# Gated delta rule: inverse of I + A with 16x16 diagonal blocks made on POOL for three steps in four

## What is computed

```python
# q, k, v [N,H,T,64], g (log-decay), beta [N,H,T]; chunks of c tokens
g = cumsum(g within the chunk)
decay = exp(where(i >= j, g_i - g_j, -inf))
a_low = where(i > j, (k*beta) @ k.T * decay, 0)
tmat = inverse(eye + a_low)                # unit lower triangular
u = tmat @ (v * beta);  w = tmat @ (k * beta * exp(g))
for each chunk:                            # the scan
    v_new = u - w @ state
    o = (q * exp(g)) @ state + (q @ k.T * decay) @ v_new
    state = state * exp(g_last) + k_dec.T @ v_new
```

## Time and profile before

| | |
|---|---|
| runs | 3808.23 us median of 3 (3802.79 to 3814.48) |
| profiled execution | 3801.48 us |
| its span | 3799.7 us |
| mean granted TensorE clock | 0.984 |
| PE busy | 3641.7 us (96%) |
| DVE, ACT, POOL busy | 1549.1, 1070.8, 1297.7 us (41%, 28%, 34%) |
| DMA | 173.19 MB, mean 46 GB/s |

### The profile page before, as it was taken

The page is one execution under the profiler, slowest core; times in us unless marked ns, Lnnn a source line. Parts: engine busy times, 40 slices in busy tenths (PEclk is TensorE's granted clock), DMA queues, the critical chain, the costliest instruction groups (busy, mean ns, idle before and its releaser), DMA issues. The chain is left out here.

```text
span 3799.7 us, 47903 instructions
## 1 busy us (share of the span) xinstructions
PE 3641.7 (96%) x19176; PEld 3016.4 (79%) x19176; DVE 1549.1 (41%) x2391; ACT 1070.8 (28%) x1817; POOL 1297.7 (34%) x876
## 2 busy tenths in 40 slices
PE   6999999999999999999999999999979999999998
PEld 5777878776898989888877787887867887777877
DVE  4332333343354535444574333333337224444433
ACT  3343333331333333333013111111121114443221
POOL 4221212124221221222345343433342435554543
PEclk9999999999999999999999999999989999999999
DMA  2000000002000000001131111111132111111122
GB/s 98 23 29 27 28 23 33 24 28 76 29 12 12 1 23 1 23 1 60 67 127 59 50 44 50 44 50 44 50 116 70 48 43 49 48 47 46 61 83 72
DMA packets 52699, 173.19 MB, mean 46 GB/s; under 512 B 6569, under 2 KB 13353, under 8 KB 49841
## 3 DMA queue, kind: packets, MB, share of 16 engines
q1 hardware_dynamic: 52528, 170.80, 13.1%
HBM read 151.25 MB, written 19.52 MB: 45 GB/s over the span
## 5 line engine op out<-in xcount | busy, mean ns | idle before, releaser
L303 PE MATMUL DP<-XH,WH 128*128 128x512 f32 x2608 | 896.4, 425 | 21.7 <-POOL WL L251 20.5
L249 POOL CAST WH<-WRAW 128x1024 fp32r<-128x1024 f32 (+2 forms) x257 | 263.8, 1026 | 1638.3 <-issue 1041.5
L303 PE MATMUL DP<-XL,WH 128*128 128x512 f32 x2608 | 812.3, 393 | 0.0
L303 PE MATMUL DP<-XH,WL 128*128 128x512 f32 x2608 | 810.3, 392 | 0.0
L303 PEld LDWEIGHTS DP<-XH,WH 128*128 128x128 f32 x2608 | 475.0, 191 | 180.5 <-issue 86.8
L251 POOL TENSOR_TENSOR WL<-WRAW,WH 128x1024 fp32r<-128x1024 f32 (+2 forms) x257 | 588.5, 2290 | 20.7
L303 PEld LDWEIGHTS DP<-XL,WH 128*128 128x128 f32 x2608 | 494.2, 190 | 107.2
L303 PEld LDWEIGHTS DP<-XH,WL 128*128 128x128 f32 x2608 | 492.7, 189 | 107.1
L836 DVE SCALAR_TENSOR_TENSOR SS<-B,RQ,SBI 128x256 f32<-128x256 f32 (+2 forms) x192 | 74.5, 429 | 380.7 <-PE B L541 380.7
L1975 POOL TENSOR_TENSOR XX<-AA,CON 128x256 f32<-128x256 f32 x64 | 45.4, 731 | 433.4 <-ACT AA L1610 433.4
L1390 PE MATMUL DP<-PM,XX 128*128 128x64 f32 (+1 forms) x1536 | 172.6, 269 | 15.4 <-ACT XX L1623 15.0
(11 more groups left out here) (461 smaller groups left out, 5497.9 us busy)
## 6 DMA issues: line engine op xcount, KB each, us to landing
WRAW<-in_w_up SPq DMA_DIRECT2D x44, 512.0 KB, 3.2
WRAW<-in_w_attn SPq DMA_DIRECT2D x36, 512.0 KB, 3.2
WRAW<-in_w_down SPq DMA_DIRECT2D x22, 512.0 KB, 3.2
XR<-in_x SPq DMA_DIRECT2D x8, 1024.0 KB, 8.0
WRAW<-in_w_dn SPq DMA_DIRECT2D x16, 512.0 KB, 3.5
WRAW<-in_w_lrux SPq DMA_DIRECT2D x10, 512.0 KB, 3.3
WRAW<-in_w_lrug SPq DMA_DIRECT2D x10, 512.0 KB, 3.2
WRAW<-in_w_bl SPq DMA_DIRECT2D x10, 512.0 KB, 3.5
```

What stands on the lines that cost most here:

```text
L249: pool.tensor_copy(WH[b.slot][:, 0:b.kt, :], WRAW[b.slot][:, 0:b.kt, :]).then_inc(w_hi, 1)
L303: mm = pe.matmul(DP[b.slot][:, half * H:half * H + H], w[b.slot][:, k, :], x[:, k, half * H:half * H + H], start=one, stop=end)
```

## The change

Step m = 0 of each round is as before, with six levels. For m = 1..3 the levels 0, 1 and 2 are left out (NB = 3, `lowest`), since Y starts there with the inverses of the 16x16 diagonal blocks. These are made in a chain of their own, twelve times (three a round):

1. Once `take_a` has stored AA of both groups of the coming step (one tile AAV of 4 KB a partition), SP writes it to memory (aa_dram, 512 KB).
2. SP loads the diagonal blocks with eight DMAs (one for each matrix q), each 8 blocks of 16 rows of 64 bytes, onto 8 partitions each: four matrices of one direction to partitions 0 to 31 of BL, four to 32 to 63 of BW.
3. POOL (`base_blocks`) turns and negates them (three instructions of 32 partitions x 256), sets the diagonal, then for j = 1..14 does a multiply and a subtract on 64 partitions x j x (15 - j) elements, each waiting for the one before, and one last copy.
4. SP stores the results with eight DMAs of the same shape to yy_dram, waits for them, and loads the whole of Y (YYV, 512 KB) from there.

`times_a` of the first level waits for that load. SP's waits are in this order in its queue, behind the loads of blocks dn 2 and 3 of the round and 0 and 1 of the next. yy_dram is zeroed once by a DMA from YYV[1], which DVE has set to zero; that DMA waits for `st_zero` and stands ahead of the load of block dn 2 of round 0.

The matrices are made earlier: for step 1, `spread_g`, `gram` and `turn_a` stand at q 0, 2, 4 and 6 of step 0; for step 2 `spread_g` and `gram` stand at q 8 to 11 of step 0, and `turn_a` and `take_a` at q 0 of step 1 (q counts from the first level that is done); for step 3 `spread_g` and `gram` at q 2 to 5 of step 1 and `turn_a` at q 0 of step 2. DQX has 10 places instead of 8; XX has one buffer for each e instead of two. `first_level` and `turn_x0` are done for m = 0 alone. POOL's `add_other` of groups 4 and 5 now stands behind each of the two splits. In `mx_fill` the order of the four fills differs.

```diff
-        DQX = at("DQX", 96, [P, 8, 2, 2, P])
+        DQX = at("DQX", 96, [P, 10, 2, 2, P])
+        AAV = [at(f"AA{v}", 120 - 4 * v, [P, 2, 2, 2, P]) for v in range(2)]
+        YYV = [at(f"YY{v}", S0 + 38 + 4 * v, [P, 2, 2, 2, P]) for v in range(2)]
...
+        def diagonal(dram, q):
+
+            return bass.AP(dram.tensor, dram.offset + P * q, ap=[[16 * (8 * P + 1), 8], [8 * P, 16], [1, 16]])
+
+        def blocks_sp(sp, g):
+
+            c, v = chain(g), g % 2
+            sp.wait_ge(aa_ready, 2 * g + 2)
+            sp.dma_start(aa_dram, AAV[v][:, :, :, :, :].rearrange("p d e h n -> p (d e h) n")).then_inc(aa_out, 16)
+            sp.wait_ge(aa_out, AA0 + 16 * (c + 1))
+            sp.wait_ge(yy_out, YYO0 + 128 * c)
+            for q in range(8):
+                t = BW if q >= 4 else BL
+                sp.dma_start(t[8 * q:8 * q + 8, :, :], diagonal(aa_dram, q)).then_inc(blk_in, 16)
+            if c:
+                sp.wait_ge(yy_in, YYI0 + 16 * c)
+            sp.wait_ge(blk_ready, RDY0 + c + 1)
+            for q in range(8):
+                t = BW if q >= 4 else BY
+                sp.dma_start(diagonal(yy_dram, q), t[8 * q:8 * q + 8, :, :]).then_inc(yy_out, 16)
+            sp.wait_ge(yy_out, YYO0 + 128 * (c + 1))
+            sp.wait_ge(v_ps, 2 * g - 2)
+            sp.dma_start(YYV[v][:, :, :, :, :].rearrange("p d e h n -> p (d e h) n"), yy_dram).then_inc(yy_in, 16)
...
             def times_a(n, l):
...
                 if l == 0:
-                    pe.wait_ge(y0_ready, n + 1)
-                if n // 2 * NL + l:
-                    pe.wait_ge(ly_ready[e], n // 2 * NL + l)
+                    pe.wait_ge(y0_ready, n // 8 * 2 + e + 1)
+                elif l == lowest(n):
+                    pe.wait_ge(yy_in, YYI0 + 16 * (chain(n // 2) + 1))
+                if levels_done(n, l):
+                    pe.wait_ge(ly_ready[e], levels_done(n, l))
...
-                if m < 3:
-                    n = NT * p + 2 * m + 2
+                n = NT * p + 2 * m + 2
+                if m == 0:
                     if q == 0:
                         spread_g(n)
-                    if q == 1:
                         spread_g(n + 1)
-                    if q == 3:
+                    if q == 2:
                         gram(n, 0)
-                    if q == 5:
+                    if q == 4:
                         gram(n, 1)
-                    if q == 7:
+                    if q == 6:
                         turn_a(n)
                         turn_a(n + 1)
...
+                if m in (1, 2) and q == 0:
+                    turn_a(n)
+                    turn_a(n + 1)
...
-                    for l in range(NL):
+                    for l in range(lowest(a), NL):
+                        q = 2 * (l - lowest(a))
...
+            def base_blocks(g):
+
+                p, c = g // 4, chain(g)
+                lo, up = slice(0, 32), slice(32, 64)
+                pool.wait_ge(blk_in, BLK0 + 128 * (c + 1))
+                pool.tensor_scalar(BY[lo, :, :], BL[lo, :, :].rearrange("p i j -> p j i"), -1.0, None, ALU.mult).then_inc(
+                    blk_step, 1)
...
+                pool.tensor_scalar(BY[up, :, :], BW[up, :, :], -1.0, None, ALU.mult).then_inc(blk_step, 1)
+                pool.tensor_copy(BL[up, :, :], BW[up, :, :].rearrange("p i j -> p j i")).then_inc(blk_step, 1)
...
+                pool.tensor_copy(BY[0:64, :, :].rearrange("p i j -> p (i j)")[:, 0:256:17], ONES[0:64, 0:16]).then_inc(
+                    blk_step, 1)
+                pool.wait_ge(blk_step, step(p, c, 4))
+                for j in range(1, 15):
+                    y = BY[0:64, 0:j, j + 1:16]
+                    t = BT[0:64, 0:j, j + 1:16]
+                    pool.tensor_tensor(t, BY[0:64, 0:j, j:j + 1].broadcast_to([64, j, 15 - j]),
+                                       BL[0:64, j + 1:16, j:j + 1].rearrange("p i a -> p a i").broadcast_to(
+                                           [64, j, 15 - j]), ALU.mult).then_inc(blk_step, 1)
+                    pool.wait_ge(blk_step, step(p, c, 2 * j + 3))
+                    pool.tensor_tensor(y, y, t, ALU.subtract).then_inc(blk_step, 1)
+                    pool.wait_ge(blk_step, step(p, c, 2 * j + 4))
+                pool.tensor_copy(BW[up, :, :], BY[up, :, :].rearrange("p i j -> p j i")).then_inc(blk_ready, 1)
+                pool.wait_ge(blk_ready, RDY0 + c + 1)
...
-                for m in range(4):
-                    prepare(NT * p + 2 * m)
-                add_other(NT * p + 4)
-                add_other(NT * p + 5)
+                for i in range(2):
+                    first_level(NT * p + i)
+                for i in range(2, 4):
+                    spread(NT * p + i)
+                for m in range(1, 4):
+                    for n in range(NT * p + 2 * m + 2, min(NT * p + 2 * m + 4, NGRP)):
+                        spread(n)
+                    base_blocks(4 * p + m)
                 for i in range(2):
                     split(pool, Block("dn", p + 1, i) if p < NPAIR - 1 else Block("mixga", 0, i))
+                    add_other(NT * p + 4 + i)
...
+                sp.wait_ge(st_zero, 1)
+                sp.dma_start(yy_dram, YYV[1][:, :, :, :, :].rearrange("p d e h n -> p (d e h) n")).then_inc(yy_out, 16)
                 for p in range(NPAIR):
-                    for i in range(0 if p else 2, 4):
+                    for i in range(2, 4):
                         load(sp, Block("dn", p, i), a["w_dn"])
...
+                    for m in range(1, 4):
+                        blocks_sp(sp, 4 * p + m)
```

More of the change, by code:

```diff
@@ L1124, in dk, with lowest, levels_done, turns_done @@
         def dk(n):
-            return DQX[:, 2 + n // 2 % 3 * 2 + n % 2]
+            return DQX[:, 2 + n // 2 % 4 * 2 + n % 2]
+        def lowest(n):
+            return 0 if n // 2 % 4 == 0 else NB
+        def levels_done(n, l):
+            m = n // 2 % 4
+            return n // 8 * LV + (NL + (m - 1) * (NL - NB) if m else 0) + l - lowest(n)
+        def turns_done(n, l):
+            m = n // 2 % 4
+            return n // 8 * TV + (NL - 1 + (m - 1) * (NL - NB) if m else 0) + l - max(lowest(n), 1)
+        def chain(g):
+            return g // 4 * 3 + g % 4 - 1
+        def diagonal(dram, q):
[18 more added lines that the diff above has]
+            sp.dma_start(YYV[v][:, :, :, :, :].rearrange("p d e h n -> p (d e h) n"), yy_dram).then_inc(yy_in, 16)
         def both_parts(n, d, h):
@@ L1149, in halves @@
             row = whole.ap[0]
-            return bass.AP(whole.tensor, whole.offset + b, ap=[[row[0], row[1]], [2 * P - b, 2], [2 * b, P // b], [1, b]])
+            return bass.AP(whole.tensor, whole.offset + b, ap=[[row[0], row[1]], [4 * P - b, 2], [2 * b, P // b], [1, b]])
         def turn_of(n, d):
@@ L1669, in between @@
                         values(a + 1)
-                if m < 3:
-                    n = NT * p + 2 * m + 2
-                    if q == 2:
+                n = NT * p + 2 * m + 2
+                if m == 0:
+                    if q == 1:
                         exponential(n)
-                    if q == 3:
                         exponential(n + 1)
-                    if q == 7:
+                    if q == 6:
                         take_a(n)
                         take_a(n + 1)
[L1679 to L1682, removed]
+                    if q == 9:
+                        exponential(n + 2)
+                        exponential(n + 3)
+                if m in (1, 2) and q == 0:
+                    take_a(n)
+                    take_a(n + 1)
+                if m == 1 and q == 3:
+                    exponential(n + 2)
+                    exponential(n + 3)
             for p in range(NPAIR):
@@ L1724, in delta_act @@
                             take_x(a + 1, l)
[L1725 to L1726 removed]
+                        between(p, m, q)
+                        between(p, m, q + 1)
                     if m == 0 and p in (1, 2):
@@ L1909, in delta_dve @@
                     dve.wait_ge(qs_ready, NT * p)
+                if p == 0:
+                    dve.memset(YYV[1][:, :, :, :, :], 0.0)
                 dve.memset(SB[:, :, :], 0.0).then_inc(st_zero, 1)
@@ L1968, in spread, with step @@
                 x.then_inc(rb_ready, 1)
+            def step(p, c, i):
+                return 2 * (p + 1) + NSTEP * c + i
             def first_level(n):
                 p, s, e, v = grp(n)
+                k = step(p - 1, 3 * p, e + 1)
                 pool.wait_ge(aa_ready, n + 1)
                 for d in range(2):
-                    x = pool.tensor_tensor(XX[v][e][:, d], AA[v][e][:, d], twice(con("m0", d, P)), ALU.mult)
+                    x = pool.tensor_tensor(XX[e][:, d], AA[v][e][:, d], twice(con("m0", d, P)), ALU.mult)
```

146 lines of the change are left out of this document (86 added, 60 removed).

## The result

The changed kernel takes 3839.5 us (median of 5 runs, 3834.29 to 3845.83) against 3808.19: a ratio of 1.0086, 95% interval 1.0069 to 1.0104. The medians are 31 us apart, 0.8%. 64 us slower had been forecast, with a range that holds the value. The profiled execution has a span of 3841.8 us, 42 more than that of before; it lies 4 us above its median, the one of before 7 us under its own. All medians are of undisturbed runs: one of the four of experiment 1 took 5802.89 us at a granted clock of 0.55 and is left out.

What follows compares the result with a forecast made beforehand. PE was taken to bound the kernel, with a chain replacing its work: 15.5 us more a round, 62 in four rounds, plus 2 for zeroing, +64 us on 3808.2 gives 3872 us, range 3812 to 3960.

Steps and rivals of the forecast that it cites:

- What bounds, and what replaces it: Inverse stage: PE work sets each step; by PE alone the kernel takes 180 us less, but the chain replaces it.
- L: Length of the chain from the last take_a stored to PE's start of the step: 30.5 us.
- POOL's part: POOL's instructions and waits within the chain: 13.2 us, bounds 8.4 and 18.9.
- the price of eight DMAs in a row: Block loads and stores on SP, spaced 0.50 us: 5.4 us in, 5.1 us out.
- The point at which the change is even: Chain length at which the changed kernel is neither faster nor slower: L = 25.3 us.
- When the chain can start: AA ready 23.6 us into step 0, 7.0 into steps 1 and 2, or 9.3 with the low clock.
- The clock: Half clock for 5 us behind PE's waits before steps 1 to 3: 7.1 us a round, bounds 0 and twice that.
- Zeroing: Round 0's load of block dn 2 comes late behind the zeroing DMA: 2 us once (0 to 4).
- The whole sum: Four inverse rounds 62 us longer plus 2 us once: +64 us, median 3872 us.
- The short chain: Rival: cheap POOL instructions and small DMAs bring L to 22.0 us, kernel 3770 us; chance of faster 0.10.
- the dear small runs: Rival: block transfers in short runs land late, L 41.8 us, median 4008 us; chance of over 3950: 0.17.
- Its rule for POOL reads with a long step: POOL reads stepping over 8 bytes cost more: an estimated 1.1 us a chain, kernel 13 us slower than the sum.

Runs made afterwards that it cites:

- experiment 1: Changed kernel without POOL's 28 multiply and subtract instructions, both trips through memory and all waits kept, Y no inverse: 3724.1 us, ratio 0.9773.
- experiment 2: Changed kernel without the whole chain, PE waiting for AA alone, levels 0 to 2 still left out, output not the reference's: 3634.9 us, ratio 0.9529.
- experiment 3: Changed kernel with 66, 50 and 66 identity matmuls added ahead of the first times_a of steps 1, 2 and 3: 3816.2 us, ratio 1.0021.
- Experiment 6: Changed kernel with turn_a and take_a of the next step at q 1 instead of q 0 in steps 1 and 2: 3868.0 us, ratio 1.0152.
- experiment 5: Changed kernel with the zeroing DMA issued behind the loads of blocks dn 2 and 3 of round 0: 3838.6 us, ratio 1.0079.
- Experiment 4: Changed kernel with two block DMAs each way instead of eight, AA and Y moved in runs of 512 bytes: 3817.9 us, ratio 1.0027.
- experiment 8: Changed kernel with 8x8 blocks instead of 16x16, two DMAs each way and the zeroing DMA behind round 0's loads: 3741.7 us, ratio 0.9828.

## Why the prediction was right, and where its size was off

- **What bounds, and what replaces it.** PE set the steps before and the chain sets them now: right, and shown by experiments 1 and 2. The PE work of the four steps is 33.4, 23.0, 19.1 and 18.2 us at full clock (the busy times above less what the low clock adds, about 2.9, 2.9 and 2.3), for 33, 23, 19 and 18.5; without a chain the change is worth 174 us, for 180. PE's busy time fell by 129 us and not by 150 to 180, since its matmuls at the low clock took 30 us longer (experiment 2).
- **The chain.** This is the term that was mis-sized most: L is 28.2 us in the mean, not 30.5, which times 12 makes the forecast 28 us too high. POOL's part was right to 0.2 us: the instructions of 14 to 56 elements take 0.21 to 0.31 us, as the start of 0.185 and 2.1 ns an element say, with 0.08 between dependent ones. What was wrong is the price of eight DMAs in a row: the spacing of 0.50 us, borrowed from transfers of 32 KB, is 0.36 here, and blocks in and out together took 8.2 us, not 10.5. The point at which the change is even, L = 25.3, was thus nearer than it looked: the direction hung on 2.9 us a chain, and an error like that of the DMAs on POOL's term as well would nearly have turned it.
- **When the chain can start.** Step 0: 23.0 us instead of 23.6. Steps 1 and 2: 10.1 in round 0 instead of 9.3, of which experiment 3 gives 3.3 to the clock, for 2.3 forecast, and leaves 6.8 of work; the prediction's 7.0 is 0.2 more than its own terms add up to. Experiment 6 shows that what stands ahead of take_a is paid in full.
- **The clock.** Right in kind. All twelve waits brought it to 0.50, and it was back 5 to 8 us behind them, for 5 forecast. It cost 7.1 us a round in the forecast; the runs with PE kept busy gave 23 us back, 6 a round, with the clock still down behind three waits.
- **Zeroing.** 2 us were forecast, 0 to 4, for the wait alone; the wait was 2.5, but with the lower clock behind it, which the term left out, it costs 6.0 in the trace (experiment 5).
- **The whole sum.** Of the 62 us forecast for the four rounds 33 came. The rounds of the changed kernel take 596.1 us, 23 less than forecast: 28 less by the chains, 5 more by the rest. Those of before had been put at four times round 0, 556.8 us, and take 562.9. With 6 for the zeroing and 3 that were not assigned this is the 42 us between the two profiled executions; their medians are 31 apart. So some of the 33 us by which the forecast was too high came from terms of opposite sign, and that L alone nearly makes them up is in part chance.
- **Rivals.** The short chain would have needed 8.4 us on POOL; the dear small runs would have needed landings of 7.4 us. By the chain's parts neither happened: the last of eight 8 KB loads was issued at about 1045.2 and POOL started at 1046.86, 1.7 us later, for runs of 64 bytes. Experiment 4 moves 32 KB a DMA in runs of 64 bytes, which those of 32 KB in the earlier trace rows move in runs of 512 by the code: 1.9 and 2.4 us to landing for the loads (1.9 in the earlier trace rows), 1.7 and 1.9 for the stores (1.6). So the Trainium skill's threshold of 512 bytes (DMA: Bandwidth & Descriptors, Specifications) cost at most 0.5 us a landing here. Its rule for POOL reads with a long step (GPSIMD Engine Reference, Performance pitfalls for Q7 kernels) is borne out in part: the turned read of 256 elements at 64 bytes took 1.07 us where the straight one of the next instruction took 0.84, 0.9 ns more an element, but the short multiplies, whose second operand is read at that step, were at most 0.02 us longer than the subtracts of the same size, which read none.

## What to carry to other kernels

Work taken off the bounding engine is worth its full time only while the chain that replaces it is shorter than what the engine has left to do from the chain's start: find that start and that remainder in the timeline before counting the gain. Such a chain is tuned at its own parts, each worth its time times the number of chains; the best cut (16x16 to 8x8 blocks) gave work back to the engine that was waiting. Here an idle PE costs twice, once in the wait and once in the half clock behind it, and the second part grows where the slowed work is what starts the next chain.

## What the runs showed that was not expected

- A wait of PE of 2.0 us was enough for the clock to fall (experiment 1). From 1066.0 to 1079.4 us PE was busy throughout at a granted clock of 1.00; it was 0.96 from there to 1081.5, the wait, and 0.50 in the 6.5 us behind, though PE was at work again. The first group took 3.68 us instead of 1.95, and 3.67 or 3.68 behind the waits of 2.4 to 2.5 us of the other rounds as well.
- SP issues DMAs of 8 KB with 128 runs every 0.36 us, and the sixteen of 32 KB in the earlier trace rows, with 64 runs each by the code, every 0.53 us. With 512 runs, the issue of one took 0.30 to 0.49 us in round 0 of experiment 4 (32 partitions) and 0.59 to 0.66 in that of experiment 8 (64 partitions). So the number of runs alone does not set it. What does was not tried.
- A store or load of 512 KB in runs of 512 bytes took 3.2 and 3.9 us, and 2.6 and 3.3 us in runs of 4 KB.
